# Projecting the samples' queries first, putting every prompt piece into the page slots, and reading window-state values page by page

## Time and profile before

| | us |
|---|---|
| median of 3 runs | 1072.36 (1069.6 to 1074.74) |
| profiled execution | 1075.88 |
| its span | 1074.2 |
| PE busy | 951.3 |
| DVE busy | 667.1 |
| ACT busy | 517.2 |
| POOL busy | 289.1 |

### The profile page before, as it was taken

The page is one execution under the profiler, slowest core; times in us unless marked ns, Lnnn a source line. Parts: engine busy times, 40 slices in busy tenths (PEclk is TensorE's granted clock), DMA queues, the critical chain, the costliest instruction groups (busy, mean ns, idle before and its releaser), DMA issues.

```text
span 1074.2 us, 29350 instructions
## 1 busy us (share of the span) xinstructions
PE 951.3 (89%) x11042; PEld 846.5 (79%) x11042; DVE 667.1 (62%) x1632; ACT 517.2 (48%) x1128; POOL 289.1 (27%) x351
## 2 busy tenths in 40 slices
PE   3989899899977789898996567899999999999996
PEld 3978788788855567676775444899999999999996
DVE  5279745676469978863564254888888888700004
ACT  6554533375226559664332652554555555611114
POOL 1321154545533355335553000000000000133331
PEclk8999999899989989999999688999999999999998
DMA  8799999999999999889998995578687786975642
GB/s 239 256 306 342 328 326 377 355 370 369 382 368 363 355 369 344 303 312 385 378 280 225 239 222 155 209 258 328 235 310 273 266 319 227 336 246 170 219 149 88
DMA packets 158165, 310.99 MB, mean 290 GB/s; under 512 B 13985, under 2 KB 88098, under 8 KB 157026
## 3 DMA queue, kind: packets, MB, share of 16 engines
q1 hardware_dynamic: 133922, 233.92, 63.0%
q0 software_dynamic: 22400, 72.37, 19.2%
q10 hardware_dynamic: 1728, 3.15, 1.2%
HBM read 302.31 MB, written 73.92 MB: 350 GB/s over the span
## 4 chain that ended last, share of the span: by engine, by line
PE 37%; issue 31%; DMA 15%; DVE 7%; ACT 4%; POOL 2%; SPq 2%; POOLq 1%; ACTq 0%; DVEq 0%
PE ps L1468 11%; PE ps L1102 8%; DMA v_ring<-in_cache_v_diff 8%; PE ps L1333 4%; DMA v_ring<-in_state_v_win 4%; PE ps L1296 4%; DMA k_ring<-in_cache_k_diff 3%; DVE kt_sb L2271 2%; PE ps L1253 2%; PE ps L1179 1%; DVE prob L2163 1%; PE ps L1350 1%; PE ps L1163 1%; PE ps L1148 1%; POOL v_ring L697 1%
## 5 line engine op out<-in xcount | busy, mean ns | idle before, releaser
L2271 DVE STREAM_TRANSPOSE kt_sb<-k_ring 128x512 f32<-128x512 f32 x336 | 219.5, 689 | 73.3 <-DMA k_ring<-in_cache_k_diff 35.5
L697 POOL DMA_DIRECT2D v_ring<-in_cache_v_diff x248 | 136.8, 553 | 154.6 <-issue 83.8
L1041 POOL TENSOR_TENSOR c_lo<-c_raw,c_hi 128x1408 fp32r<-128x1408 f32 x14 | 46.7, 3337 | 416.1 <-ACT c_hi L1884 416.1
L1102 PE MATMUL ps<-h_hi,w_hi 128*128 128x288 f32 x384 | 124.2, 323 | 1.9 <-DVE h_lo L2125 1.9
L1102 PE MATMUL ps<-h_lo,w_hi 128*128 128x288 f32 x384 | 115.1, 300 | 0.0
L1102 PE MATMUL ps<-h_hi,w_lo 128*128 128x288 f32 x384 | 114.8, 299 | 0.0
L1333 PE MATMUL ps<-v_ring,pt_sb 128*32 128x128 f32 x2240 | 80.5, 286 | 33.5 <-DMA v_ring<-in_cache_v_diff 21.6
L1296 PE MATMUL ps<-kt_sb,q_st 128*32 128x128 f32 (+1 forms) x2816 | 95.0, 277 | 6.9 <-DVE q_st L2281 4.1
L997 POOL TENSOR_TENSOR w_lo<-w_raw,w_hi 128x1024 fp32r<-128x1024 f32 x24 | 57.3, 2388 | 152.0 <-ACT w_hi L1585 152.0
L1333 PEld LDWEIGHTS ps<-v_ring,pt_sb 128*32 128x32 f32 x2240 | 62.6, 114 | 45.2 <-issue 41.6
L1296 PEld LDWEIGHTS ps<-kt_sb,q_st 128*32 128x32 f32 x2816 | 71.6, 112 | 24.0 <-issue 17.1
(11 more groups left out here) (248 smaller groups left out, 2354.2 us busy)
## 6 DMA issues: line engine op xcount, KB each, us to landing
k_ring<-in_cache_k_diff SPq DMA_DIRECT2D x256, 256.0 KB, 6.8
v_ring<-in_cache_v_diff POOLq DMA_DIRECT2D x248, 256.0 KB, 6.7
out_k_win_sample<-in_state_k_win SPq DMA_DIRECT2D x32, 1020.0 KB, 8.3
out_v_win_sample<-in_state_v_win SPq DMA_DIRECT2D x32, 1020.0 KB, 8.0
k_ring<-in_state_k_win SPq DMA_DIRECT2D x40, 512.0 KB, 7.0
w_raw<-in_w_in SPq DMA_DIRECT2D x24, 512.0 KB, 7.5
g_raw<-in_w_gate SPq DMA_DIRECT2D x11, 1024.0 KB, 5.3
g_raw<-in_w_up SPq DMA_DIRECT2D x11, 1024.0 KB, 5.4
```

What stands on the lines that cost most here:

```text
L697: queue.dma_start(dst, src.rearrange("(b j) c -> j b c", b=4))\
L1041: nc.gpsimd.tensor_tensor(c_lo[j][:, 0:width], c_raw[:, j, 0:width], c_hi[j][:, 0:width].bitcast(F32), ALU.subtract).then_inc(w_lo_done, 1)
L1102: last = nc.tensor.matmul(M[c][:, 0:HALF], wt, act[:, k, c * HALF:(c + 1) * HALF], start=k == 0 and at_first, stop=k == KT - 1 and act is ...
L2271: V.transpose(kt_sb[:, i, :], k_ring[:, i, :]).then_inc(kt_done, 1)
```

## The change

- `PRE` is 0: all 316 pieces lie in the slots, with new numbers in `SHARE`.
- The norm takes the samples' block first (`NORM_ORDER`). As soon as it is in `h_hi`, PE projects the four query tiles of A for the 64 sample columns alone (`project_samples`, into one PSUM bank), ACT copies and turns them (`copy_sample_queries`), DVE rotates them (`rope_sample_queries`), and item 0's queries are laid out. The first four weight chunks have four buffers, all loaded and split at the start. In tiles 0 to 3 `project` then leaves the samples' columns out: its second half has 224 columns.
- ACT's queue loads the prompt blocks of x. The page table comes with the norm's constants, and the pages of slot 0 no longer wait for the other constants.
- Item 3's queries go into buffer 0 at the end of slot 23, in one go.
- The four shift copies of sequence 0's keys move from the prelude to the down projection.
- The first two slots of a B item take all 128 rows x 4 positions. Each value load is one position of 128 rows, placed like a page; the third slot's loads are cut as 16 rows x 4 positions.

```diff
-FETCH_AT = {23: 3, 30: 4, 33: 5, 36: 6, 39: 7}
+FETCH_AT = {30: 4, 33: 5, 36: 6, 39: 7}
-PRE = 36
+PRE = 0
-SHARE = [6] * 8 + [8] * 14 + [5] * 20 + [4, 4] + [3] * 4 + [0] * (SLOTS - 48)
+SHARE = ([9] * 8 + [8] * 14 + [6] * 4 + [5] + [6] * 5 + [7] + [5, 5, 6] + [5, 5] + [4] * 10
+         + [0] * (SLOTS - 48))
...
             if pages_of(q) == 4:
-                return state[2 * (it - 4) + b, 64 * g:64 * g + 64, 0:8, :]
+                return state[2 * (it - 4) + b, :, 4 * g:4 * g + 4, :]
             return state[2 * (it - 4) + b, 96:P, 8:16, :]
...
-                rows = slice(0, P) if pages_of(q) == 4 else slice(64 * s, 64 * s + 64)
-                src = state_rows(sv, q, s).rearrange("(b a) i c -> b a i c", b=4)[b]
+                if pages_of(q) == 4:
+                    place_page(queue, q, i, state_rows(sv, q, s)[:, b, :])
+                    continue
+                rows = slice(64 * s, 64 * s + 64)
+                src = state_rows(sv, q, s).rearrange("(r a) (u i) c -> u r a i c", r=2, u=2)[b // 2, b % 2]
...
-                    if j == 4 and n < COPIES:
-                        shift_window(*shifts.pop(0))
...
                 shift_window("k_win", 3 + m // 4, m % 4)
+                if m % 2:
+                    shift_window("k_win", 0, m // 2)
...
+                cols = slice(c * HALF, SEQ if n < 4 and c else (c + 1) * HALF)
                 for k in (2 * kk, 2 * kk + 1):
...
-                        last = nc.tensor.matmul(M[c][:, 0:HALF], wt, act[:, k, c * HALF:(c + 1) * HALF],
+                        last = nc.tensor.matmul(M[c][:, 0:cols.stop - cols.start], wt, act[:, k, cols],
...
+            def project_samples(n):
+
+                pe.wait_ge(w_lo_done, n + 1)
+                pe.wait_ge(hlo_done, 2)
+                for k in range(KT):
+                    w = slice(k * P, k * P + P)
+                    for wt, act, at_first in ((hi_at(n)[:, w], h_hi, True), (hi_at(n)[:, w], h_lo, False),
+                                              (lo_at(n)[:, w], h_hi, False)):
+                        last = nc.tensor.matmul(Z[1][:, n * NS:n * NS + NS], wt, act[:, k, SEQ:NT],
+                                                start=k == 0 and at_first, stop=k == KT - 1 and act is h_hi and not at_first)
+                last.then_inc(qs_projected, 1)
...
+            norm_transposes(0, NORM_ORDER[0])
+            project_samples(0)
+            project_samples(1)
+            norm_transposes(1, NORM_ORDER[1])
+            project_samples(2)
+            norm_transposes(2, NORM_ORDER[2])
+            project_samples(3)
+            norm_transposes(3, NORM_ORDER[3])
+            norm_transposes(4, NORM_ORDER[4])
...
+            def copy_sample_queries():
+
+                act.wait_ge(qs_projected, 4)
+                cols = slice(0, 4 * NS)
+                nc.scalar.activation(feat[:, 1, cols], Z[1][:, cols], ACT.Copy).then_inc(qs_turned, 1)
+                act.wait_ge(qs_turned, 1)
+                for q in range(4):
+                    s = slice(32 * q, 32 * q + 32)
+                    d = slice(32 * (q ^ 1), 32 * (q ^ 1) + 32)
+                    last = nc.scalar.activation(rot[d, cols], feat[s, 1, cols], ACT.Copy)
+                last.then_inc(qs_turned, 1)
...
-                    if i == 7 and t + 1 in FIRST[1:3]:
+                    if i == 7 and t + 1 in FIRST[1:4]:
                         fetch_q(FIRST.index(t + 1))
```

More of the change, by code:

```diff
@@ L743, in raw_count, with place_pair @@
             return n * 8 + (16 - 8 * par)
-        def state_pair(state, q, i):
-            n, k = pages_of(q), i % 4
-            return state_rows(state, q, i // 4).rearrange("p (s x) c -> p s x c", x=n)[:, :, k - 1:k + 1, :]
+        def place_pair(queue, q, i):
+            rows, k = state_rows(sk, q, i // 4), i % 4
+            if pages_of(q) == 4:
+                queue.dma_start(k_ring[:, i - 1:i + 1, :], rows[:, k - 1:k + 1, :]).then_inc(k_landed[i], 16)
+            else:
+                for u in range(2):
+                    src = rows[:, 4 * u:4 * u + 4, :].rearrange("p (s x) c -> p s x c", x=2)
+                    queue.dma_start(k_ring[64 * u:64 * u + 64, i - 1:i + 1, :], src).then_inc(k_landed[i], 16)
         @block.sync
@@ L846, in load_values @@
                 values_of_group(sp, t, h, first_ids)
-            sp.wait_ge(const_in, 16 * N_CONST)
-            for i in range(8):
-                load_keys(0, i)
             def store_k(n):
@@ L2126, in norm_lo, with rope_sample_queries, mean, rows @@
                                     hi[s].bitcast(F32), ALU.subtract).then_inc(hlo_done, 1)
-            def norm_blocks():
-                for blk in range(NBLK):
-                    norm_mean(blk, blk)
-                    if blk:
-                        norm_rows(blk - 1, blk - 1)
-                norm_lo(0, 0, h_hi, h_lo)
-                norm_rows(NBLK - 1, NBLK - 1)
-                for blk in range(1, NBLK):
-                    norm_lo(blk, blk, h_hi, h_lo)
+            def rope_sample_queries():
+                dve.wait_ge(const_in, 16 * N_CONST)
+                dve.wait_ge(qs_turned, 2)
+                for f in range(4):
+                    s = slice(f * NS, f * NS + NS)
+                    V.tensor_tensor(feat[:, 1, s], feat[:, 1, s], rope_cs[:, 0, SEQ:NT], ALU.mult)
+                    last = V.tensor_tensor(rot[:, s], rot[:, s], rope_cs[:, 1, SEQ:NT], ALU.mult)
+                last.then_inc(rope_parts, 2)
+                dve.wait_ge(rope_parts, 2)
+                for f in range(4):
+                    s = slice(f * NS, f * NS + NS)
+                    V.tensor_tensor(q_s[:, f, :], feat[:, 1, s], rot[:, s], ALU.add).then_inc(rope_s_done, 1)
+            def norm_blocks():
+                def mean(u):
+                    norm_mean(u, NORM_ORDER[u])
+                def rows(u):
+                    norm_rows(u, NORM_ORDER[u])
+                def low(u):
+                    norm_lo(u, NORM_ORDER[u], h_hi, h_lo)
+                mean(0)
+                rows(0)
+                low(0)
+                mean(1)
+                rows(1)
+                mean(2)
+                rows(2)
+                low(1)
+                mean(3)
+                rows(3)
+                mean(4)
+                low(2)
+                rows(4)
+                rope_sample_queries()
+                low(3)
+                fetch_first_q()
+                low(4)
             def rope(n):
@@ L2482, in _ @@
             V.memset(zero, 0.0).then_inc(sign_step, 1)
-            for p in range(PRE):
-                main(p)
             dve.wait_ge(sign_step, 2)
```

207 lines of the change are left out of this document (116 added, 91 removed).

## The result

The changed kernel takes 1101.41 us (median of 4 runs, 1097.33 to 1105.73), the kernel before 1070.98 us beside it (4 runs). The ratio on record is 1.0247, 95% interval 1.0204 to 1.029 (the two medians alone would give 1.028, 4 us more). The forecast was 1048 and the range ended at 1083. The profiled execution took 1099.57 us, its span 1097.9.

A forecast was written before the change was run, and what follows sets the result against it. Limits by stage: PE, DVE and DMA nearly full in slots 1 to 7, DMA in 8 to 21, state values at 545 to 661 us, PE from about 700. Terms -10 +4 +1 +2 +0 -22 = -25 gave 1048 us; range 1036 to 1083.

The forecast's parts named there:

- The 96 matmuls of 64 columns are 3 to 10 us in a stretch where PE mostly waits: Samples' projections ahead of slot 0: cheap at 3 to 10 us, with PE beginning slot 0 at about 36 us.
- The straight line: Matmul time by width, drawn through 288 columns (0.143 us) and 512 (0.249); gives about 0.11 us for 224 columns.
- Slots 32 to 43: 57 against 58: Pieces held by these slots after and before the change; nearly equal, so no time change was counted.
- Slots 8 to 21: Slots with 8 pieces before and after, taken as limited by DMA: change 0.
- The term for slots 22 to 31: 59 pieces instead of 50, half hidden: +4 us, bounds 0 and +9; item 3's queries in one go add +2.
- State values -22: State stage, 545 to 661 us: single-page value reads run faster, -22 us taken of 23 + 12, bounds -32 and 0.
- The two-page groups: Four 1 MB state groups re-cut to 16 rows by 4: each could win 3 us; extra key issues cost 0.
- slots 0 to 7 once begun: Slots 0 to 7 with 72 pieces: 77 us of PE work from 36 us, ending at 116 with waits; -10 us.
- the copies at 0: Four window copies moved from the first 60 us to the down projection: 0, bounds -3 and +3.
- Rival 1: Narrow matmuls in first four tiles of slots 0 to 3 run at plain f32 rate: +23.5 us, 1071; chance 0.24.
- Rival 2: State values stay as slow as they are, or another wait takes over: +22 us, 1070; chance 0.14.
- Rival 3: State values come slower, engines reading in step 64 KB and 1 MB apart: 1088 with some hidden; chance 0.14.

The follow-up runs named there:

- e3: The kernel before with 320 more matmuls ahead of its first piece, eight runs of 40 at widths 288 to 32; 64 columns: 112 ns full clock, 213 half.
- e5: The changed kernel with the samples' queries from the high x high product alone, 64 of the 96 narrow matmuls left out; 1086.89 us, ratio 1.0137.
- e9: The changed kernel with 84 pieces in slots 0 to 7 and the shares of the kernel before from slot 8 on; 1084.41 us, ratio 1.0104.
- e4: The changed kernel with 5 pieces in each of slots 22 to 41 as before, the rest in slots 42 to 47; 1100.41 us, ratio 1.0303.
- e2: The changed kernel with the old reading of the states put back; 1104.87 us, ratio 1.0319.
- e6: The changed kernel with the prompt's norm transposes ahead of the samples' projections as far as inputs allow; 1106.76 us, ratio 1.0324.
- e12: The kernel before with the new state reading for the first two slots of a B item alone; 1062.21 us, ratio 0.9897.
- e13: The kernel before with the third slots of the B items alone cut anew, values and keys; 1076.16 us, ratio 1.0023.
- e7: The kernel before with the new state reading and the four shift copies moved to the down projection; 1070.57 us, ratio 0.9959.
- e10: e9 with item 3's queries spread over slot 23 into the second buffer as before; 1083.13 us, ratio 1.0084.

## Why the prediction was wrong

- **"The 96 matmuls of 64 columns are 3 to 10 us in a stretch where PE mostly waits"** failed, in size and in place. They are 20.4 us (chain; e3 gives the 213 ns; e5 takes 64 of them out and gets 12 to 14.5 us back), and PE is the engine on which the chain stands from 16.75 us on. The straight line through 288 and 512 columns was carried on to 64, where e3 shows a floor. That it gave the right 0.11 us for 224 columns was luck: e3 has 111 to 112 ns for all of 224, 192, 128 and 64, so 224 stands on the floor already and not on the line. The text had put a last group at "3 to 5 us" at the cold clock, which is right (24 x 213 ns = 5.1 us), and did not count the three before it nor the transposes queued between them. That is 13.5 of the front's 16 us; the wait in slot 7 (2.4 us), which the prediction didn't name, is the rest.
- **"Slots 32 to 43: 57 against 58", so 0,** failed as a way of counting: it compares numbers of pieces and not which piece meets which slot. Slot 32 alone is 10.7 us longer. The prediction priced a piece at 0.9 us as if all were projection; those in slot 32 are attention, with narrow matmuls, and meet slots other than before. e9 shows that the placing is the cause, e4 that the number per slot isn't. By the rows of slot 32 in five kernels 7 of the 10.7 us are the half clock and 4 the pieces. What made the clock fall there is open. Slots 8 to 21, at 0 as well, took 3.6 us more; nine traces with the pieces of before take 182.6 to 186.1 there, and those of the changed kernel, e2, e4, e5 and e6, 12 pieces behind, 185.1 to 192.6, so a few us of it are real. The term for slots 22 to 31, +4 and +2 for the queries, was right: 5.7 us in the ledger, 7 by the means of all traces.
- **"State values -22"** had the direction and the rate right (345 GB/s instead of some 260) and the size wrong. Split by e12 and e13: the four-page groups give 11 us, not 23, because PE's waits for these values were 22.7 us in all and ACT's weights are late next; "what is late next" named PE and SP's issues, and not ACT. The two-page groups, which the prediction let win up to 3 us each, with their keys at 0, win nothing: e13 is at +0.2% (interval -0.03 to +0.48%), and their keys slow slots 36 to 39. The Trainium skill (DMA: Bandwidth & Descriptors, "Why a DMA increments its semaphore by 16 and not by 1") gives the new cut of these values 16 engines instead of 8. The trace agrees on the engines: before, the share behind slot 43 has two stretches at 5 tenths, and in e13 it is 9 tenths in every slice from 599.8 to 657 us. It doesn't bear out a gain: the rate is 223 GB/s on the mean (599.8 to 666.0 us in e13) against 220 (595.5 to 661.0 before).
- Right: the 224-column time (by the luck told above); slots 0 to 7 once begun (82 us for 80); the copies at 0 (e7, within its noise); item 3's queries, in so far as e10 can't tell 2 us from 0. Rival 1 didn't happen. Rival 2 had "or another wait takes over", and that half of it did: the values came fast, and ACT's wait took over part of the gain. Rival 3 had the four-page values "slower than before", and their rate rose; it was the two-page keys that came slower. Its distances, 64 KB and 1 MB, come out of no row, and no run shows which engine reads which row. Rival 1's price was mis-added: 0.376 less 0.11 is 0.266 and not 0.245 us, 25.5 us in all.
- The miss as a whole: 16 (front) + 3.6 (slots 8 to 21) + 18.4 (32 to 39, of which 10.7 in slot 32 and 5.6 in 36 to 39) + 11 (state) = 49 us, the distance from -25 to +24.

## What to carry to other kernels

A projection for few columns is paid per matmul, not per column: count its matmuls at the spacing that the narrowest width of this operand shows, at both levels of the clock (here 112 and 213 ns), and see whether PE is the engine everybody waits for there. When work is dealt to slots, an equal number per slot is not an equal slot: list which pieces meet which slot, and keep the alignment that the old shares had when pieces are moved ahead. And split a re-cut read by the groups it touches before it is timed: here one half won 11 us, and the other won nothing and made four slots 6 us longer.

## What the runs showed of the hardware

- The spacing of matmuls that each load 128 x 128 weights of this kind has a floor: 111 to 112 ns for 224 down to 64 columns at 2.4 GHz, 213 ns for 64 and 32 at 1.2 GHz (e3). The Trainium skill (TensorE: Matmul & The Clock Gate, "Back-to-back issue gap") gives N / 2.4 GHz + 2.5 ns for an isolated one, 56 ns at 128 columns, and about 81 ns in a stream with weight loads; this trace has 112, so neither holds for these operands.
- The granted clock fell to half at 55.0 us, in a run of 64-column matmuls issued without a gap, stayed there under 32 columns, and rose at 68.6 us under 288 columns (e3).
- In the first stage of the changed kernel (16.7 to 27.2 us) the profile prints PEclk 1.00, while 64-column matmuls stand 213 ns apart, as at PEclk 0.50 in e3. Its first record of the clock is at 43.3 us. Ahead of that record the spacing tells the clock better than the column.
- With the same pieces, slot 32 took 24.8, 23.2 and 21.5 us at PEclk 0.72, 0.78 and 0.84: 18 us each at the full clock.
- Two cuts of the same state rows, both in runs of 4 KB, go with 389 and with mostly 181 to 250 GB/s while they land, the engines equally full (e12, e13). Why the halved loads are slow, the runs don't show.
